# Where the adaLN sums run, and how the token shift of the first projection is made

## Reference

```python
mod = silu(c) @ w_ada + b_ada                       # [1024] @ [1024, 6144], one row
shift_m, scale_m, gate_m, shift_f, scale_f, gate_f = split(mod, 6)
h = rms_norm(x, g_pre_mix) * (1 + scale_m) + shift_m    # 256 tokens x 1024
p = h @ w_in                                        # 54 tiles of 128 columns
p_shift, pq, pk_att, pv_att, p_ga, p_gb = split(p, ...)   # p_shift: the first 20 tiles
p_shift = p_shift + mu_shift * (token_shift(p_shift) - p_shift)   # token_shift: the token before, 0 for the first
```

## Time and profile before

| | us |
|---|---|
| median of 3 runs (2142.82 to 2150.68) | 2144.09 |
| profiled execution, its own time | 2144.94 |
| its span in the profile | 2142.9 |
| busy: TensorE / VectorE / ScalarE / GpSimd | 1988.7 / 1404.7 / 898.7 / 128.5 |
| first stage (first matmul of the projection to the barrier) | 41.1 to 197.2 |

### The profile page before, as it was taken

The page is one execution under the profiler, slowest core; times in us unless marked ns, Lnnn a source line. Parts: engine busy times, 40 slices in busy tenths (PEclk is TensorE's granted clock), DMA queues, the critical chain, the costliest instruction groups (busy, mean ns, idle before and its releaser), DMA issues.

```text
span 2142.9 us, 37023 instructions
## 1 busy us (share of the span) xinstructions
PE 1988.7 (93%) x14932; PEld 1909.4 (89%) x14932; DVE 1404.7 (66%) x2184; ACT 898.7 (42%) x1328; POOL 128.5 (6%) x182
## 2 busy tenths in 40 slices
PE   7898798996799999999999899999999999889997
PEld 6897688984699999998889889999999878889997
DVE  6865576765756557755755767756775565667774
ACT  3223254332455444443445454444444354444442
POOL 0520022200000000001100000000000200000000
PEclk7998798987899999999999999999999999999999
DMA  8565110002445535553323435543554322354552
GB/s 339 216 259 180 40 60 1 2 1 61 158 157 176 209 126 172 172 192 109 112 79 121 136 136 173 180 182 133 172 181 172 120 97 99 99 177 141 193 194 101
DMA packets 43447, 301.40 MB, mean 141 GB/s; under 512 B 4736, under 2 KB 6928, under 8 KB 11072
## 3 DMA queue, kind: packets, MB, share of 16 engines
q1 hardware_dynamic: 42736, 296.90, 39.8%
q0 software_dynamic: 592, 2.87, 0.4%
HBM read 298.70 MB, written 1.05 MB: 140 GB/s over the span
## 4 chain that ended last, share of the span: by engine, by line
PE 78%; DVE 10%; DVEq 4%; ACT 3%; issue 2%; DMA 2%; POOL 0%; ACTq 0%; POOLq 0%; SPq 0%
PE acc L696 20%; PE acc L698 20%; PE acc L697 20%; DVE w_lo L667 2%; ACT w_hi L660 2%; PE mb L824 2%; PE acc L2559 2%; PE mb L719 1%; PE mb L1967 1%; PE acc L1967 1%; DVEq L1403 1%; PE mb L2531 1%; DMA land<-in_w_out 1%; PE mb L1964 1%; DVE gla_sq L2897 1%
## 5 line engine op out<-in xcount | busy, mean ns | idle before, releaser
L696 PE MATMUL acc<-h_hi,w_hi 128*128 128x272 f32 (+1 forms) x2960 | 875.6, 296 | 45.4 <-DVE w_lo L667 19.5
L697 PE MATMUL acc<-h_lo,w_hi 128*128 128x272 f32 (+1 forms) x2960 | 858.2, 290 | 0.0
L698 PE MATMUL acc<-h_hi,w_lo 128*128 128x272 f32 (+1 forms) x2960 | 856.3, 289 | 0.0
L667 DVE TENSOR_TENSOR w_lo<-land,w_hi 128x2048 fp32r<-128x2048 f32 (+2 forms) x251 | 576.9, 2299 | 203.0 <-ACT w_hi L660 202.7
L660 ACT ACTIVATE w_hi<-land 128x2048 fp32r<-128x2048 f32 (+2 forms) x251 | 481.8, 1920 | 523.0 <-PE acc L698 461.6
L696 PEld LDWEIGHTS acc<-h_hi,w_hi 128*128 128x128 f32 x2960 | 571.8, 193 | 59.1 <-DVE w_lo L667 21.7
L697 PEld LDWEIGHTS acc<-h_lo,w_hi 128*128 128x128 f32 x2960 | 573.2, 194 | 2.0 <-issue 0.2
L698 PEld LDWEIGHTS acc<-h_hi,w_lo 128*128 128x128 f32 x2960 | 573.9, 194 | 0.0
L696 PE MATMUL acc<-a_hi,w_hi 128*128 128x272 f32 (+1 forms) x880 | 252.3, 287 | 0.6 <-DVE w_lo L667 0.3
L698 PE MATMUL acc<-a_hi,w_lo 128*128 128x272 f32 (+1 forms) x880 | 252.4, 287 | 0.0
L697 PE MATMUL acc<-a_lo,w_hi 128*128 128x272 f32 (+1 forms) x880 | 251.4, 286 | 0.0
(11 more groups left out here) (519 smaller groups left out, 2589.7 us busy)
## 6 DMA issues: line engine op xcount, KB each, us to landing
land<-in_w_gu SPq DMA_DIRECT2D x110, 1024.0 KB, 4.9
land<-in_w_in SPq DMA_DIRECT2D x65, 1024.0 KB, 4.9
land<-in_w_down SPq DMA_DIRECT2D x40, 1408.0 KB, 6.0
ada_first<-in_w_ada SPq DMA_DIRECT2D x24, 1024.0 KB, 8.6
land<-in_w_ab SPq DMA_DIRECT2D x24, 512.0 KB, 3.5
land<-in_w_out SPq DMA_DIRECT2D x12, 1024.0 KB, 4.9
land<-in_w_in_single SPq DMA_DIRECT2D x6, 512.0 KB, 3.5
const<-in_const POOLq DMA_DIRECT2D x1, 1134.0 KB, 7.9
```

The costliest lines, as they stand in the source:

```text
L667: k.nc.vector.tensor_tensor(k.w_lo[:, p.par, 0:size * P], k.land[:, p.par, 0:size * P], k.w_hi[:, p.par, 0:size * P].bitcast(F32), ALU.sub ...
L696: mm(out, k.w_hi[:, par, c], hi, start=start, stop=False)
L697: mm(out, k.w_hi[:, par, c], lo, start=False, stop=False)
L698: return mm(out, k.w_lo[:, par, c], hi, start=False, stop=stop)
```

## The change

It does three things. All later adaLN panels (n = 8 to 23) are summed on VectorE; the first ones that TensorE takes whole are still 1, 3 and 5, but the step of 4 now comes ahead of the whole of 5. The token shift is written as (1 - mu) * p + mu * (p of the token before): ScalarE evacuates each of the two accumulator tiles of a panel twice, once scaled by `mu` into a buffer of `c1` (three in turn) and once scaled by `kept` = 1 - mu into `p_in`. GpSimd then adds the first to `p_in` one column further with one operation. Before it overwrites a buffer, ScalarE waits until GpSimd has read it (`shifted`). `kept` is made once by VectorE at the start. The loops of ScalarE and GpSimd over the ten pairs are unrolled.

```diff
-ADA_TENSOR = (1, 3, 5) + tuple(ADA_FIRST + j for j in range(2, ADA_LATER, 4))
-ADA_ORDER = (1, 0, 3, 2, 5, 4, 6, 7) + tuple(range(ADA_FIRST, 24))
+ADA_TENSOR = (1, 3, 5)
+ADA_ORDER = (1, 0, 3, 2, 4, 5, 6, 7) + tuple(range(ADA_FIRST, 24))
...
+MOVED = RT // 2
+
+def moved_tiles(k, i):
+    return k.c1[:, 2 * (i % MOVED):2 * (i % MOVED) + 2, :]
+
+def act_shifted(k, act):
+    a = k.nc.scalar.activation
+    def one(i, p, _):
+        ahead(split_hi, k, act, p, "same", IN_K)
+        act.wait_ge(k.panel_done, p.count(3))
+        if i >= MOVED:
+            act.wait_ge(k.shifted, i - MOVED + 1)
+        for o in range(2):
+            t = 2 * i + o
+            a(moved_tiles(k, i)[:, o, :], k.acc[:, 2 * p.par + o, 0:SEQ], ACT.Copy, scale=vec(k, "mu", t))
+            last = a(k.p_in[:, t, 1:SEQ + 1], k.acc[:, 2 * p.par + o, 0:SEQ], ACT.Copy, scale=k.kept[:, t:t + 1])
+        last.then_inc(k.acc_free, 1)
+        act.drain().then_inc(k.pin_ready, 1)
+    section(act, 0, SHIFT_TILES // 2, one, unrolled=True)
+
 def pool_shift(k, pool):
     g = k.nc.gpsimd
-    with pool.Fori(0, SHIFT_TILES // 2) as i:
+    for i in range(SHIFT_TILES // 2):
         pool.wait_ge(k.pin_ready, i + 1)
-        two = bass.ds(i * 2, 2)
-        g.tensor_tensor(k.c1[:, 0:2, :], k.p_in[:, two, 0:SEQ], k.p_in[:, two, 1:SEQ + 1], ALU.subtract)
-        pool.drain()
-        mu = k.vec[:, bass.ds(i * 2 + VEC["mu"][0], 2)].unsqueeze(2).broadcast_to([P, 2, SEQ])
-        g.tensor_tensor(k.c1[:, 0:2, :], k.c1[:, 0:2, :], mu, ALU.mult)
-        pool.drain()
-        g.tensor_tensor(k.p_in[:, two, 1:SEQ + 1], k.p_in[:, two, 1:SEQ + 1], k.c1[:, 0:2, :], ALU.add)
-        pool.drain()
+        p = k.p_in[:, 2 * i:2 * i + 2, 2:SEQ + 1]
+        g.tensor_tensor(p, p, moved_tiles(k, i)[:, :, 0:SEQ - 1], ALU.add).then_inc(k.shifted, 1)
+    pool.drain()
...
-    act_copy_out(k, act, 0, 10, 2, lambda i: k.p_in[:, bass.ds(i * 2, 2), 1:SEQ + 1], SEQ, IN_K, (IN_K, IN_K),
-                 signal=k.pin_ready)
+    act_shifted(k, act)
...
+    v.tensor_scalar(k.kept[:, :], vec(k, "mu", n=SHIFT_TILES), -1.0, 1.0, ALU.mult, ALU.add)
     v.tensor_scalar(k.csil_mean[:, :], k.csil[:, :], 1.0 / D, None, ALU.mult).then_inc(k.csig, 1)
```

More of the change, by code:

```diff
@@ L249, in allocate @@
     k.warm = fixed("warm", [P, 8])
+    k.kept = fixed("kept", [P, SHIFT_TILES])
     h_at = where[0]
@@ L470, in semaphores @@
     k.prep_ready = sem("prep_ready")
+    k.shifted = sem("shifted")
     k.xbd_ready = sem("xbd_ready")
```

## The result

The changed kernel takes 2122.18 us (median of 6 runs, 2112.88 to 2123.36) against 2143.53 for the kernel before (6 runs, 2140.33 to 2150.68). The ratio of the runs is 0.9891, with a 95% interval from 0.9873 to 0.9909: 1.1% faster (the two medians alone divide to 0.9900). The prediction was 2118.2, 1.2% faster, and the range 2110 to 2127 holds the measured time. The profiled execution went from a span of 2142.9 to one of 2119.9 us.

The account below looks back on a forecast made before the run. TensorE was taken to set the time over the span, with waits for VectorE in the first stage. Gain 187.4 - 160.5 = 26.9 us, less 1 for the clock: 2144.09 - 25.9 = 2118.2 us; range 2110 to 2127.

Parts of the forecast that it names:

- Start: Order of the first sums: VectorE's wait before n = 7 goes but the usual 0.2 us; gain 2.4 us.
- Whole panels: First stage: four whole panels leave TensorE, removing 17.6 us and 6.0 us of low-clock stretches, adding 1.4 us of column steps.
- GpSimd's add: VectorE's rounds beside GpSimd: one add of 1.30 us costs VectorE 0.88 us, between 0 and 2.1.
- ScalarE: Evacuation in the ten pair rounds: four operations take 1.0 to 1.4 us more, covered by 1.9 us of slack; cost 0.
- The walk along the splits: VectorE's splits in the first stage: panel 10 at 107.65, panel 19 at 160.5 instead of 187.43; gain 26.9 us.
- TensorE's waits: Rounds that VectorE bounds: TensorE idles 1.27 us a round, some 9 us in all.
- Clock: Level rounds of the first stage: 1 us taken off the gain for a fall of the clock.
- rival B: First stage, dearer rounds: the add costs 2.1 us (2129), or the clock falls in waiting and level rounds (2123); chance 0.16.
- To the end: After the first stage: all later work hangs on its closing barrier, so the gain of 25.9 us should reach the end.
- rival C: Later stages start in another phase of clock and loads and take back over 15 us: 2135; chance 0.06.
- D: Slower: the clock stays at 1.2 GHz through the first stage, 41 us more, 2185; loses above 8.18 a round; chance 0.03.
- a sign of being wrong: First stage: the prediction called itself wrong if, among other signs, `w_hi` waits for a landing.

Follow-up runs that it names:

- e_order: Kernel before with only the order changed, the step of n = 4 ahead of panel 5; a single run, 2150.51 us beside 2147.68 for the kernel before.
- e_shift: Kernel after with the two lists of before, so TensorE again takes n = 10, 14, 18, 22 whole; 2138.32 us, ratio 0.9953 to the kernel before.
- e_one_evac: Kernel after with one unscaled 512-column evacuation in place of four of 256, token shift left out; median 2116.59 us, ratio 0.9868 to the kernel before.
- e_sums: Kernel before with only the two lists changed: later sums on VectorE, new order, GpSimd's three operations kept; 2137.5 us, ratio 0.9948.
- e_two_adds: Kernel after with GpSimd's add made twice, so the shifted half counts double; 2132.38 us, ratio 0.9932 to the kernel before.
- e_after_again: Kernel after, unchanged, run once more on the same chip as a later version; 2123.36 us, ratio 0.9878 to the kernel before.

## Why the prediction was nearly right

*Start: wrong in size.* It took 2.4 us of gain; the profile of the kernel after shows 41.14 - 40.47 = 0.7, with the sum of n = 7 at 32.01 and not near 30.2. The step that failed is "goes but the usual 0.2 us": that wait did go (0.16 before the sum of n = 7), but waits of 1.24 and 1.85 came up at n = 4 and n = 6, which I had not looked for, since I had taken TensorE's times in the start as fixed. Where the clock fell late (`e_order`), the gain was 2.0.

*Whole panels: right.* Their stretches at low clock are gone from the stage after, and `e_shift`, which keeps them, has them still. The prediction took the 3.4 us of the first for all four; in the trace of before the third and fourth last 6.8 and 6.9 us, but they begin within the panel, and 3.9 and 3.7 us of them lie behind it.

*GpSimd's add: right in price, off by one in count.* 0.88 was taken for each, and 0.85 is measured, 0.93 where a round has one alone. The walk put one add into each of the eight rounds; they hold nine, which makes their mean 7.49 and not 7.41. The loss of 0.67 per us of GpSimd, read from one round with three operations, is no constant: an add of 1.32 us (69.33) lengthened one of VectorE's pairs by 1.91 - 0.88 = 1.03, while the one of 2.80 us (57.54) lengthened a pair behind it (59.37) by only 1.39 - 0.62 = 0.77. That add began during the split of 56.92. The split took its usual 2.29 us, and the add ended 1.1 us after it; the adds of 51.35 and 114.21 also began during a split, and ended 1.0 and 1.1 us after theirs. An add takes 1.13 us beside a sum (76.87), so here it was GpSimd that was held up. By the rule that the prediction takes from the Trainium skill ("SBUF — State Buffer", section "Who interferes with whom"), that the other engine fully blocks for the whole instruction, VectorE would lose the whole length of an add that comes first. The trace agrees where the split comes first. Where the add falls on a sum, as in the six rounds with one add, VectorE loses less than the add's row is long: 0.83 us for rows of 1.13 to 1.23 us, 1.03 for 1.32 to 1.59. Whether that is sharing, or a row that is longer than the block, no run here shows.

*ScalarE: right.* Cost 0: 3.9 us of idle time remain behind the evacuation (`e_one_evac`). The operations overlap, so the extra time was 0.97 us, at the low end of the 1.0 to 1.4 of the estimate.

*The walk along the splits.* The split of panel 10 was set at 107.65 and is at 109.70: 1.44 late from the start (49.81 for 48.37), 0.61 from the rounds. That of panel 11 is at 112.67 for 110.3, that of 19 at 162.88 for 160.5, 2.4 late: 1.4 of it start, 0.6 the ninth add, and 0.3 that came in at panel 11. The six level rounds were set at 6.53, and are 6.52. The gain there is thus 187.43 - 162.88 = 24.55 and not 26.9.

*TensorE's waits: right.* Some 9 us at 1.27 a round were forecast; 9.1 at up to 1.3 came.

*Clock: wrong, by little.* I took 1 us for a fall in the level rounds; there was none from 43.6 to 169.9. The rule in "TensorE: Matmul & The Clock Gate" (the Trainium skill, section "HAM oscillation — how this bites in real kernels") needs waits long enough, and the 1.07 to 1.31 us in seven rounds of 7.4 were not. In `e_sums`, with waits of up to 1.6 us for a split and 2.0 for a sum, the clock fell four times. The length of one wait doesn't decide it alone: in `e_two_adds` the clock fell at 70.1 and 87.2, behind waits of 1.59 us (ended 69.19 and 85.87), and not behind those of 2.67 and 1.60 us that ended at 61.16 and 102.55. In `e_after_again` it fell once, 68.4 to 71.8, and the splits did not move for it: as argued for rival B, in a round that VectorE bounds, TensorE's idle time takes it up.

*To the end.* From 24.8 us at the stage's end 23.0 are left. The difference, 1.8, is in the later stages, which had 5 us more at low clock; at 0.43 that is 2.2. This is no part of the change, since the same code ranges over 28 us between profiles. So rival C, the gain given back, did not happen beyond that spread; D needed a mean round over 8.18, and the rounds were 7.49 and 6.52. One thing that the prediction named as a sign of being wrong did come: `w_hi` waited for a landing, once, for 4.2 us (73.39). It had no effect, since the split of that panel began only at 79.86.

In sum: 26.9 - 2.4 (start, ninth add, panel 11) = 24.5 at the split of panel 19, 24.8 at the next stage's first matmul, no clock loss, and 1.8 less in the later stages give the 23.0 of the span. Of the change's own terms the start was furthest off. The median is 4.0 us above the forecast: 2.9 of it is this (25.9 - 23.0), and 1.1 is that the profiled execution of before lay 0.9 us above its median and that of after 0.2 below.

## What to carry to other kernels

Find the engine that bounds each round, not the span: here TensorE was 93% busy, and it paid to take 17.6 us of work from it and let it idle 9, because VectorE's rounds were nearly level once GpSimd disturbed it less. An operation given to GpSimd isn't free for VectorE; compare what it steals (0.93 us) with what it would take there (0.59). Idle time that is spread in small pieces took a small piece well (half a us more for each column step, beside the adds) and a lump of 4.9 us not at all.

## What was not expected of the hardware

- The same later stages took 1930.6 to 1959.1 us from profile to profile, 0.43 us for each us at 1.2 GHz. For a change of this size only the repeated runs and the distance inside one stage can be compared.
- When the clock falls in the whole panels of the start differs by 2.6 us from profile to profile (16.3 to 18.9 us with the new order), and moves the first matmul by 1.7 us. TensorE was busy then with matmuls of one column. What in those sets the moment stays open.
- An add of GpSimd that began during one of VectorE's splits ended 1.0 to 1.1 us after the split, whether it began late or early in it (51.35, 57.54 and 114.21 in the kernel after, 1.71, 2.80 and 1.90 us long), and the split kept its 2.29 us.
- A landing came late once in the stage (4.2 us of ScalarE's time in the kernel after) and cost no round: the split is made ahead.
